# Hybrid conv / S5 / PEER layer: order of the weight tiles ahead of the experts, who issues the small inputs, where the taps stand, the conv tiles' SiLU, and when gate batches are loaded

## The chip, the cores and the metric

The kernel runs on one core of a Trainium2 chip. The metric is the device time of one execution in microseconds (us). The core has five engines, each with its own instruction stream: TensorE (PE, matmuls), VectorE (DVE), ScalarE (ACT), GpSimd (POOL) and SyncE (SP, which here only issues DMAs). They meet through semaphores only.

## The reference, cut to what matters

One layer of a decoder trunk on 512 prompt positions and 8 single-token sequences (T = 520 columns), D = 1024:

```
mods = silu(c) @ w_ada + b_ada                  # 6 x 1024, and 2 x 1024 for the final norm
h = rms_norm(x) * (1 + sc1) + sh1
a, gate, u = split(h @ w_in, [512, 1024])       # 12 tiles of 128 output rows
hc = causal_depthwise_conv(a * sigmoid(gate), width 31)
hc = silu(layer_norm(hc))
hs = glu(gelu(s5_scan(u)), w_glu)               # 32 groups, 64 complex states each
x += g1 * (concat(hc, hs) @ w_out)
h2 = rms_norm(x) * (1 + sc2) + sh2
q = h2 @ w_q; scores = q . keys                 # 8 heads x 2 x 128 keys
idx, g = top-16 of the 16 x 16 best pairs of each head
x += g2 * sum_k g_k * gelu(h2 . U[idx_k]) * V[idx_k]
y = rms_norm(x) * (1 + scf) + shf
```

The last sum is computed densely over all 16384 experts for the first 384 columns (gates are written as a table, most of them zero), and by gathered rows for the other 136.

## The kernel before

Activations lie as columns: partitions are features, the free axis is the 520 tokens. Every weight tile is 128 x 1024 f32 (512 KB) and comes through `raw`, a ring of four places. `STREAM` lists the 96 tiles ahead of the experts in the order in which SyncE asks for them: `("in", f)`, `("glu", f)`, `("out", f)`, `("q", f)` and `("ada", f)`, the modulation tiles, 16 to each of four pairs. Tile n waits until tile n - 4 has been used (`USED`): an `ada` tile when its matmuls are done, an `in`, `out` or `q` tile when its low part is computed.

Dense products are made in two parts for precision: ScalarE copies a tile rounded (`split_hi`), VectorE or GpSimd subtracts to get the rest (`split_lo`), into a ring of two (`hlm`, later `hl`), and TensorE multiplies three combinations (`split_dense`): 48 matmuls of 256 or 264 columns per tile.

The order of work ahead of the experts is written out by hand, engine by engine. The input projection (`split_dense("in", ...)`) makes 12 tiles; after tiles 1, 3, 5 and 7 it calls `modulation_rows(1, ...)` for four `ada` tiles. VectorE computes between its splits the S5 factors (`XI`, `FO`), then for each pair of gate and value tiles the GLU rows (`conv_rows`, which TensorE waits for at tiles 7, 9 and 11), and part of the 124 convolution taps (`conv_taps(count, tiles)`). After the projection come small chunk matrices (20 steps of TensorE and ScalarE), chunk inputs (`s_V`), the scan on VectorE that ends in the chunk states `S` (semaphore `s_S`), the direct chunks on TensorE, which wait for the second modulations (`s_mods`), the S5 outputs, the GLU, and on VectorE the rest of the taps. Then the layer norm: TensorE sums columns, VectorE takes reciprocals, ScalarE the root (`root("conv")`), VectorE multiplies, ScalarE applies SiLU with the permutation of columns (`natural`) and copies the rounded part (`rhi`), VectorE subtracts (`rows_lo`, into `mixin_lo`). Then the output projection, the second norm, `modulation_rows(3, ...)`, the q projection, and scores in five token tiles, which ScalarE copies from PSUM in four pieces each.

The experts: 128 tiles of U (`first_product`), then 128 of V, 16 batches of eight. For the V half SyncE loads the activations (`hring`, four places) and the gates by batches of 1.5 MB (`load_gates`, two places, `gbp`); VectorE multiplies both (`weigh`) eight tiles ahead of TensorE, and the engine's next instructions, `row_weights` (`Wd`) and `add_out`, stand behind it. Gathered activations come into `ga` with `VG` = 2 semaphores in turn.

## Time and profile before

| | before |
|---|---|
| median of 3 runs | 1979.05 us (1974.23 to 1981.84) |
| profiled execution | 1975.13 us |
| its span, first to last instruction | 1973.3 us |
| mean granted TensorE clock | 0.958 |
| busy share: PE, DVE, ACT, POOL | 90%, 61%, 35%, 34% |

The profile is that of one execution. An engine's busy share says how long it had an instruction, not whether anybody waited for it; for that one reads the chain of work that ended last, and the idle time before an instruction with what released it (`<-`). The granted clock is a share of 2.4 GHz; it has two levels, 2.4 and 1.2 GHz. PEld is the weight load, which lies beside the matmuls.

### The profile page before, as it was taken

What the parts mean: (1) busy time and instruction counts of PE and PEld (TensorE: products, weight loads), DVE (VectorE), ACT (ScalarE), POOL (GpSimd) and SP (SyncE); (2) the same over time, 40 slices, a digit from 0 to 9 for tenths busy, and PEclk for the clock granted to TensorE, in tenths of its full rate; (3) what the DMA queues carried; (4) which work ended last, traced back from release to release, by engine and by line L of the source; (5) the groups of instructions that cost most, each with busy time, mean ns of one, the idle gap of its engine ahead of it and who ended that gap; (6) DMA issues with size and microseconds to landing.
All of it is one profiled execution on the core that took longest, in us unless ns stands there. A gap on an engine that the chain in (4) does not pass through costs nothing.

```text
span 1973.3 us, 32898 instructions
## 1 busy us (share of the span) xinstructions
PE 1773.7 (90%) x13007; PEld 1640.8 (83%) x13007; DVE 1195.3 (61%) x3100; ACT 686.5 (35%) x1225; POOL 673.5 (34%) x585
## 2 busy tenths in 40 slices
PE   4578638889999999999999999998999999999996
PEld 1567526679999999999999999997788887888885
DVE  5747993304999477777676671254555554655554
ACT  1213213314333444444444443332333332333333
POOL 1010001223554533333333334464344444444300
PEclk9789868899999999999999999999999999999998
DMA  7353015443888878888888887678888888888841
GB/s 243 137 161 76 12 43 180 144 171 110 237 242 240 239 218 241 261 249 245 256 248 246 252 255 243 233 273 298 308 302 311 291 294 284 311 297 317 297 151 54
DMA packets 305705, 442.68 MB, mean 224 GB/s; under 512 B 24752, under 2 KB 221536, under 8 KB 303504
## 3 DMA queue, kind: packets, MB, share of 16 engines
q1 hardware_dynamic: 275104, 365.06, 57.8%
q0 software_dynamic: 25136, 74.24, 11.4%
q8 instruction: 103, 1.69, 0.3%
q10 hardware_dynamic: 5312, 1.29, 0.3%
q14 instruction: 50, 0.41, 0.1%
HBM read 377.37 MB, written 130.25 MB: 257 GB/s over the span
## 4 chain that ended last, share of the span: by engine, by line
PE 79%; DVE 9%; DMA 7%; ACT 2%; issue 1%; ACTq 1%; POOL 0%; SPq 0%; DVEq 0%
PE ps L1707 37%; PE ps L1734 23%; PE ps L1505 9%; DMA gbp<-gate_spill 5%; PE ps L1696 4%; PE ps L1686 3%; DVE conv_out L1108 3%; DMA raw<-in_w_ada 1%; DMA raw<-in_w_in 1%; PE ps L1479 1%; PE ps L1520 1%; PE ps L1462 1%; DVE rstd L1026 1%; DVE wf L1379 0%; ACTq L640 0%
## 5 line engine op out<-in xcount | busy, mean ns | idle before, releaser
L1707 PE MATMUL ps<-h,hl 128*128 128x256 f32 (+1 forms) x6144 | 823.7, 288 | 0.0
L1707 PEld LDWEIGHTS ps<-h,hl 128*128 128x128 f32 x6144 | 761.7, 189 | 0.2 <-ACT sc L811 0.2
L1734 PEld LDWEIGHTS ps<-WH,hl 128*128 128x128 f32 x3072 | 535.2, 188 | 41.0 <-issue 26.9
L794 ACT ACTIVATE hl<-raw 128x512 fp32r<-128x512 f32 x512 | 320.7, 629 | 706.0 <-PE ps L1707 473.5
L1734 PE MATMUL ps<-WH,hl 128*128 128x384 f32 x3072 | 550.9, 339 | 6.5 <-DVE x_res L1425 5.2
L593 POOL TENSOR_TENSOR hl<-raw,hl 128x512 fp32r<-128x512 f32 x260 | 351.7, 1354 | 496.8 <-ACT hl L794 496.4
L1418 DVE TENSOR_TENSOR hl<-raw,hl 128x512 fp32r<-128x512 f32 x252 | 173.6, 694 | 212.6 <-ACT hl L794 212.5
L601 POOL DMA_INDIRECT gathered_act<-act_spill,act_index x136 | 133.8, 984 | 261.1 <-DVE Wd L1256 226.8
L1347 DVE TENSOR_SCALAR ohA<-ps,selT 128x128 f32<-128x128 f32 x384 | 134.2, 349 | 146.2 <-PE ps L1696 133.5
L1348 DVE TENSOR_SCALAR ohB<-ps,selT 128x128 f32<-128x128 f32 x384 | 154.7, 403 | 0.0
L1696 PE MATMUL ps<-ohB,ohA 128*128 128x128 f32 x768 | 147.1, 273 | 1.5 <-DVE ohB L1348 1.5
L610 POOL DMA_INDIRECT v_rows_ring<-v_rows,v_row_index x136 | 132.7, 976 | 41.5 <-issue 41.5
L1505 PE MATMUL ps<-rows_hi,hlm 128*128 128x256 f32 (+1 forms) x640 | 115.7, 303 | 34.6 <-DVE hlm L999 22.7
L847 ACT ACTIVATE WH<-wf 128x384 fp32r<-128x384 f32 x128 | 66.8, 525 | 207.0 <-DVE wf L1379 207.0
L1505 PEld LDWEIGHTS ps<-rows_hi,hlm 128*128 128x128 f32 x640 | 97.9, 206 | 40.1 <-DVE hlm L999 37.8
L1379 DVE TENSOR_TENSOR wf<-hring,gbp 128x384 f32<-128x384 f32 x128 | 74.5, 582 | 85.6 <-DMA gbp<-gate_spill 85.0
L1696 PEld LDWEIGHTS ps<-ohB,ohA 128*128 128x128 f32 x768 | 118.9, 189 | 1.7 <-ACT selT L865 1.7
L840 ACT ACTIVATE stage<-ps 128x512 f32<-128x512 f32 x96 | 102.5, 1068 | 11.8 <-PE ps L1696 11.8
L1462 PE MATMUL ps<-raw,sil 128*32 128x512 f32 x256 | 55.4, 719 | 46.3 <-DMA raw<-in_w_ada 26.6
L1686 PE MATMUL ps<-v_rows_ring,Wd 128*32 128x512 f32 x544 | 73.0, 659 | 23.5 <-DVE Wd L1256 23.5
L1425 DVE SCALAR_TENSOR_TENSOR x_res<-ps,mods,x_res 128x384 f32<-128x384 f32 x128 | 78.3, 612 | 7.6 <-PE ps L1734 7.6
L1386 DVE TENSOR_TENSOR WH<-wf,WH 128x384 fp32r<-128x384 f32 x128 | 72.6, 568 | 17.0 <-ACT WH L847 11.7
(272 smaller groups left out, 1327.6 us busy)
## 6 DMA issues: line engine op xcount, KB each, us to landing
raw<-in_u SPq DMA_DIRECT2D x128, 512.0 KB, 6.8
v_rows<-in_v SPq DMA_DIRECT2D x128, 512.0 KB, 5.7
raw<-in_v SPq DMA_DIRECT2D x128, 512.0 KB, 6.9
act_spill<-actr SPq DMA_DIRECT2D x128, 260.0 KB, 2.6
raw<-in_w_ada SPq DMA_DIRECT2D x64, 512.0 KB, 4.6
gate_spill<-stage SPq DMA_DIRECT2D x24, 1024.0 KB, 7.6
hring<-act_spill SPq DMA_DIRECT2D x128, 192.0 KB, 4.0
gbp<-gate_spill SPq DMA_DIRECT2D x16, 1536.0 KB, 8.2
```

The costliest lines, as they stand in the source:

```text
L593: pool.tensor_tensor(hl[:, n % 2, 1, c], raw[:, n % NRAW, c], hl[:, n % 2, 0, c].bitcast(F32), ALU.subtract).then_inc(s_wlo, 1)
L601: pool.indirect_dma_start(ga[:, tok:tok + 1], None, hd.rearrange("n p (t o) -> (n p t) o", o=1), bass.IndirectOffsetOnAxis(ap=ida[:, tok:t ...
L610: pool.indirect_dma_start(vring[:, g % VG, c, :], None, vrd, bass.IndirectOffsetOnAxis(ap=idv[:, tok:tok + 1], axis=0))\
L794: act.activation(hl[:, n % 2, 0, c], raw[:, n % NRAW, c], ACT.Copy).then_inc(s_whi, 1)
L1347: dve.tensor_scalar(ohA[:, s, :], ps[:, 7, 0:P], selT[:, 0, tok:tok + 1], None, ALU.is_equal)
L1348: dve.tensor_scalar(ohB[:, s, :], ps[:, 7, 0:P], selT[:, 1, tok:tok + 1], selT[:, 2, tok:tok + 1], ALU.is_equal, ALU.mult).then_inc(s_oh, 1)
L1418: dve.tensor_tensor(hl[:, n % 2, 1, c], raw[:, n % NRAW, c], hl[:, n % 2, 0, c].bitcast(F32), ALU.subtract).then_inc(s_vlo, 1)
L1505: last = pe.matmul(ps[:, bank + h, 0:b - a], ring[:, k % 2, w, q * P:(q + 1) * P], rows[r][:, q, a:b], start=i == 0 and (w, r) == (0, 0), ...
L1686: last = pe.matmul(ps[32 * c:32 * c + 32, acc_bank(s) + half, :], Wd[:, g % 2, c, :], vring[:, g % VG, c, 512 * half:512 * half + 512], st ...
L1696: pe.matmul(ps[:, 4 + g % 2, i * P:(i + 1) * P], ohA[:, tok % OHR, :], ohB[:, tok % OHR, :], start=True, stop=True).then_inc(s_tok, 1)
L1707: last = pe.matmul(ps[:, 2 * (m % 2) + h, 0:b - a], hl[:, m % 2, w, q * P:(q + 1) * P], h2[:, r, q, a:b], start=q == 0 and (w, r) == (0, 0 ...
L1734: last = pe.matmul(ps[:, mm % 2, 0:ND], hl[:, mm % 2, w, j * P:(j + 1) * P], WHL[b % 2][:, r, j, :], start=j == 0 and (w, r) == (0, 0), st ...
```

## The change

1. `STREAM` is put in the order in which TensorE uses the tiles: the 12 `in` tiles in a row, then `ada` pair 1; `out` 0 and 1 after twelve tiles of pair 2.
2. `modulation_rows(1, ...)` leaves the input projection and is done in four pieces after it; its column step and VectorE's `modulations(1)` come later. `modulation_rows(2, ...)` is cut otherwise: 2, 4 and 2 of the eight steps, the last behind output tile 0.
3. The 12 loads of small inputs are issued by SyncE after the first four weight tiles, ahead of x, and no longer by ScalarE.
4. Ten taps stand before the scan (six after the skip is added, four before the wait for the chunk inputs).
5. Conv tiles: VectorE multiplies by the root's result and permutes in one step into `mixin`, ScalarE does one SiLU over 520 columns in place, and VectorE makes the rounded copy. ScalarE's splits of `out` 0 and 1 stand behind the squares and ahead of the root.
6. ScalarE's splits of `q` 0 and 1 move into the output projection's loop.
7. Scores: ScalarE copies two pieces per token tile, VectorE the other two; the first expert product waits for both.
8. Gate batch b + 3, no longer b + 2, is loaded at the end of block b of the V half, with batch 2 at its first tile.
9. Gathered activations have four semaphores and are issued one group ahead of the gathered V rows.

```diff
@@ -69,6 +69,7 @@
 VG = 2
+GA = 4
 HR = 2
@@ -95,16 +96,12 @@
     return [(kind, f) for f in indices]
-STREAM = (ada(0, 0, KD) + tiles_of("in", 8, 9)
-          + ada(1, 0, 2) + tiles_of("in", 10, 11)
-          + ada(1, 2, 4) + tiles_of("in", 0, 4)
-          + ada(1, 4, 6) + tiles_of("in", 1, 5)
-          + ada(1, 6, 8) + tiles_of("in", 2, 6, 3, 7)
+STREAM = (ada(0, 0, KD) + tiles_of("in", 8, 9, 10, 11, 0, 4, 1, 5, 2, 6, 3, 7)
+          + ada(1, 0, KD)
           + tiles_of("glu", 0, 1, 2, 3)
-          + tiles_of("out", 0, 1) + ada(2, 0, 5)
-          + tiles_of("out", 2, 3) + ada(2, 5, 8)
-          + tiles_of("out", 4, 5, 6, 7)
-          + tiles_of("q", 0, 1) + ada(3, 0, 8)
+          + ada(2, 0, 6) + tiles_of("out", 0, 1)
+          + ada(2, 6, KD) + tiles_of("out", 2, 3, 4, 5, 6, 7)
+          + tiles_of("q", 0, 1) + ada(3, 0, KD)
           + tiles_of("q", 2, 3, 4, 5, 6, 7))
@@ -451,6 +449,11 @@
                 load(n)
+            for name, t in (("par", par[:]), ("bm", bm[:]), ("cm", cm[:]), ("h0", h0[:]),
+                            ("cw", cw[:]), ("cvec", cvec[:]), ("bada", bada[:]), ("ngain", ngain[:])):
+                sp.dma_start(t, dr[name]).then_inc(s_small, 16)
+            for c in range(CT):
+                sp.dma_start(stc[:, c, :, 0:CW - 1], dr["stc"][:, c]).then_inc(s_small, 16)
             for k in range(KD):
@@ -520,9 +523,12 @@
                 b = mm // JB
-                if mm % JB == JB - 1 and b + 2 < NB:
+                if mm == 0:
+                    sp.wait_ge(s_w, JB)
+                    load_gates(2)
+                if mm % JB == JB - 1 and b + 3 < NB:
                     sp.wait_ge(s_w, JB * (b + 2))
-                    load_gates(b + 2)
+                    load_gates(b + 3)
             sp.wait_ge(s_hs, 3 * (KD + 1))
@@ -595,12 +601,12 @@
             def gather_acts(g):
-                after(pool, s_wd, g - VG + 1)
+                after(pool, s_wd, g - GA + 1)
                 for c in range(NGT):
...
                                             bass.IndirectOffsetOnAxis(ap=ida[:, tok:tok + 1], axis=0))\
-                        .then_inc(s_ga[g % VG], 16)
+                        .then_inc(s_ga[g % GA], 16)
             def gather_v(g, c):
@@ -626,18 +632,15 @@
                 gather_v(0, c)
+            gather_acts(1)
             for g in range(1, NGG):
-                gather_acts(g)
+                if g + 1 < NGG:
+                    gather_acts(g + 1)
                 for c in range(NGT):
...
         def _(act):
-            for name, t in (("par", par[:]), ("bm", bm[:]), ("cm", cm[:]), ("h0", h0[:]),
-                            ("cw", cw[:]), ("cvec", cvec[:]), ("bada", bada[:]), ("ngain", ngain[:])):
-                act.dma_start(t, dr[name]).then_inc(s_small, 16)
-            for c in range(CT):
-                act.dma_start(stc[:, c, :, 0:CW - 1], dr["stc"][:, c]).then_inc(s_small, 16)
             act.wait_ge(s_c, 16)
@@ -698,8 +701,6 @@
                 last.then_inc(s_sig, 1)
-                if t == 2:
-                    modulation_rows(1)
             for e in range(20):
@@ -719,6 +720,8 @@
                                    ps[:, 3 * a + b, 0:(t1 - t0) * (NC + 2 * TS)], ACT.Copy).then_inc(s_Ve, 1)
+            modulation_rows(1)
+
             def chunk_outputs(e):
@@ -746,22 +749,18 @@
                 last.then_inc(s_gsig, 1)
+            act.wait_ge(s_hsm, CT)
+            act.activation(rhi[:, CT:KD, :], mixin[:, CT:KD, :], ACT.Copy).then_inc(s_rh, 1)
+
+            act.wait_ge(s_cvd, 1)
+            squares("conv", cv, CT)
             split_hi(FSP["out"], hlm)
             split_hi(FSP["out"] + 1, hlm)
-            act.wait_ge(s_hsm, CT)
-            act.activation(rhi[:, CT:KD, :], mixin[:, CT:KD, :], ACT.Copy).then_inc(s_rh, 1)
-
-            act.wait_ge(s_cvd, 1)
-            squares("conv", cv, CT)
             root("conv")
...
                 act.wait_ge(s_cn, t + 1)
-                act.activation(mixin[:, t, 0:TP].rearrange("p (i c) -> p i c", i=L), natural(cv[:, t, 0:TP]), ACT.Silu,
-                               scale=cvec[:, 1, t:t + 1], bias=cvec[:, 2, t:t + 1])
-                act.activation(mixin[:, t, TP:T], cv[:, t, TP:T], ACT.Silu,
+                act.activation(mixin[:, t, :], mixin[:, t, :], ACT.Silu,
                                scale=cvec[:, 1, t:t + 1], bias=cvec[:, 2, t:t + 1]).then_inc(s_hcm, 1)
-                act.wait_ge(s_hcm, t + 1)
-                act.activation(rhi[:, t, :], mixin[:, t, :], ACT.Copy).then_inc(s_rh, 1)
             for k in range(KD):
@@ -771,10 +770,10 @@
                 act.activation(sq[:, k % 2, :], x[:, k, :], ACT.Square).then_inc(s_sq, 1)
-                if k == 5:
+                if k == 3:
                     modulation_rows(2)
-            split_hi(FSP["q"], hl)
-            split_hi(FSP["q"] + 1, hl)
+                if k in (5, 6):
+                    split_hi(FSP["q"] + k - 5, hl)
             root("rms2")
@@ -806,7 +805,7 @@
                 act.wait_ge(s_sc, t + 1)
-                for q in range(4):
+                for q in range(2):
                     part, h4 = divmod(q, 2)
@@ -1124,7 +1123,6 @@
             conv_rows(3)
-            modulations(1)
             for i in range(5):
@@ -1135,6 +1133,7 @@
                 dve.scalar_tensor_tensor(lag0, mask, cvec[:, 3, n4:n4 + 1], lag0, ALU.mult, ALU.add).then_inc(s_dg, 1)
+            conv_taps(6, tuple(range(CT)))
             prod = wt[:, :, :].rearrange("p t c -> p (t c)")[:, 0:CT * TS * CW].rearrange(
@@ -1153,6 +1152,7 @@
                 cmul([R[:, a, :, m:2 * m] for a in (0, 1)], q, [R[:, a, :, 0:m] for a in (0, 1)], wt[:, :, 0:m])
+            conv_taps(4, tuple(range(CT)))
             dve.wait_ge(s_Ve, 6)
@@ -1167,6 +1167,7 @@
                 link(dve.tensor_tensor_scan(W2f[:, a, :], wtf, W2f[:, a, :], 0.0, ALU.mult, ALU.add))
+            modulations(1)
             dve.tensor_tensor(V[:, 0, :, 0:NC], W2[:, 0], R[:, 0], ALU.mult)
@@ -1199,10 +1197,17 @@
             dve.wait_ge(s_cvd, 1)
-            variance("conv", CC)
+            reciprocals("conv", CC)
+            split_lo(FSP["out"])
+            dve.wait_ge(s_rstd, RSTD["conv"])
             for t in range(CT):
-                dve.tensor_tensor(cv[:, t, :], cv[:, t, :], rstd[:], ALU.mult).then_inc(s_cn, 1)
+                dve.tensor_tensor(mixin[:, t, 0:TP].rearrange("p (i c) -> p i c", i=L), natural(cv[:, t, 0:TP]),
+                                  natural(rstd[:, 0:TP]), ALU.mult)
+                dve.tensor_tensor(mixin[:, t, TP:T], cv[:, t, TP:T], rstd[:, TP:T], ALU.mult).then_inc(s_cn, 1)
+            split_lo(FSP["out"] + 1)
             for t in range(CT):
+                dve.wait_ge(s_hcm, t + 1)
+                dve.tensor_copy(rhi[:, t, :], mixin[:, t, :]).then_inc(s_rh, 1)
                 rows_lo(t, t + 2)
@@ -1242,13 +1247,26 @@
             dve.wait_ge(s_h2l, KD + 1)
+
+            def scores_half(t):
+
+                dve.wait_ge(s_sc, t + 1)
+                for q in range(2, 4):
+                    part, h4 = divmod(q, 2)
+                    last = dve.tensor_copy(sc[0:size(t), t, 8 * h4 + part:8 * h4 + 8:2, :],
+                                           ps[0:size(t), 4 * (1 - t % 2) + q, :].rearrange("p (a n) -> p a n", n=NK))
+                last.then_inc(s_scd, 1)
+
+            for t in range(NTT):
+                scores_half(t)
             dve.wait_ge(s_act, NTT)
+            dve.wait_ge(s_scd, NTT)
             dve.memset(Wd[:], 0.0)
...
             def row_weights(g):
-                dve.wait_ge(s_ga[g % VG], 16 * NGT * (g // VG + 1))
+                dve.wait_ge(s_ga[g % GA], 16 * NGT * (g // GA + 1))
                 if g >= 2:
@@ -1532,14 +1550,8 @@
             modulation_columns(0)
-            def second_modulations(t):
-
-                if t % 2 and t < 8:
-                    modulation_rows(1, t - 1, t + 1)
-                if t == 9:
-                    modulation_columns(1)
-
-            split_dense("in", hlm, (rhi, h1lo), None, s_win, second_modulations)
+            split_dense("in", hlm, (rhi, h1lo), None, s_win)
+            modulation_rows(1, 0, 2)
             pe.wait_ge(s_Xr, 3)
@@ -1566,6 +1578,8 @@
                 last.then_inc(s_prep, 1)
+                if e == 15:
+                    modulation_rows(1, 2, 4)
             pe.wait_ge(s_prepe, 20)
@@ -1578,15 +1592,24 @@
             last.then_inc(s_V, 1)
+            modulation_rows(1, 4, 6)
+
             def chunk_out(t, g):
                 return ps[0:NC + TS, 4 * g + t // 4, (t % 4) * P:(t % 4 + 1) * P]
+            def direct_chunks(g, first, last_):
+
+                for t in range(first, last_):
+                    pe.matmul(chunk_out(t, g), U[:, 2 * t + g, 0:NC + TS], Tm[:, 2 * t + g, :], start=t % 4 == 0, stop=False)
+
             pe.wait_ge(s_Ve, 6)
+            direct_chunks(0, 0, ST)
+            modulation_rows(1, 6, KD)
+            direct_chunks(1, 0, ST // 2)
+            modulation_columns(1)
             pe.wait_ge(s_mods, 2)
-            for g in range(2):
-                for t in range(ST):
-                    pe.matmul(chunk_out(t, g), U[:, 2 * t + g, 0:NC + TS], Tm[:, 2 * t + g, :], start=t % 4 == 0, stop=False)
+            direct_chunks(1, ST // 2, ST)
             pe.wait_ge(s_S, 1)
@@ -1623,17 +1646,17 @@
                 last.then_inc(s_glu, 1)
-            modulation_rows(2, 0, 1)
+            modulation_rows(2, 0, 2)
             pe.wait_ge(s_cv, CT * CW)
...
             column_sums(sq_rows, CT, SQ_BEFORE["conv"], True)
-            modulation_rows(2, 1, 5)
+            modulation_rows(2, 2, 6)
             def third_modulations(t):
-                if t == 3:
-                    modulation_rows(2, 5, KD)
-                if t == 6:
+                if t == 0:
+                    modulation_rows(2, 6, KD)
+                if t == 4:
                     modulation_columns(2)
@@ -1712,6 +1736,7 @@
                         token(slot_token(m, q))
+            pe.wait_ge(s_scd, NTT)
             for m in range(NK):
```

The three places that matter most, as the instructions stand on the engines. First SyncE's queue ahead of the experts, before; each row is an instruction form with its count, `raw<-in_w_ada` a modulation tile, `raw<-in_w_in` an input projection tile.

```order
L448 DMA raw<-in_w_ada 128x1024 x12
L448 DMA raw<-in_w_in 128x1024 x2
L448 DMA raw<-in_w_ada 128x1024 x4
L448 DMA raw<-in_w_in 128x1024 x2
...
L448 DMA raw<-in_w_ada 128x1024 x4
L448 DMA raw<-in_w_in 128x1024 x4
L448 DMA raw<-in_w_glu 128x512 x4
L448 DMA raw<-in_w_out 128x1024 x2
L448 DMA raw<-in_w_ada 128x1024 x10
L448 DMA raw<-in_w_out 128x1024 x2
L448 DMA raw<-in_w_ada 128x1024 x6
L448 DMA raw<-in_w_out 128x1024 x4
```

The same queue in the changed kernel, from its beginning.

```order
L446 DMA raw<-in_w_ada 128x1024 x4
...
L454 DMA ngain_sb<-in_ngain 128x24
L456 DMA stc_sb<-in_stc 128x8x30 x4
L458 DMA x_res<-in_x 128x520 x8
L446 DMA raw<-in_w_ada 128x1024 x12
L446 DMA raw<-in_w_in 128x1024 x12
L446 DMA raw<-in_w_ada 128x1024 x16
L446 DMA raw<-in_w_glu 128x512 x4
L446 DMA raw<-in_w_ada 128x1024 x12
L446 DMA raw<-in_w_out 128x1024 x2
L446 DMA raw<-in_w_ada 128x1024 x4
L446 DMA raw<-in_w_out 128x1024 x6
```

The input projection's tiles stand in one row of 12, the eight small inputs and `stc` between the first weights and x, and the first two output tiles behind twelve modulation tiles.

Second ScalarE at the conv layer norm, before: `uT` is the GLU's sigmoid, `hlm<-raw` the split of an output tile, `sq` the squares, `rstd` the root, `mixin` the SiLU.

```order
L747 ACTIVATE uT<-ps 128x264
L655 ACTIVATE hlm<-raw 128x1024 x2
L752 ACTIVATE rows_hi<-mixin 128x2080
L661 ACTIVATE sq<-conv_out 128x520 x4
L665 ACT_TABLE_LOAD
L665 ACTIVATE rstd<-rstd 128x520
L759 ACT_TABLE_LOAD
L759 ACTIVATE mixin<-conv_out,cvec_sb 128x512
L761 ACTIVATE mixin<-conv_out,cvec_sb 128x8
L764 ACTIVATE rows_hi<-mixin 128x520
```

And in the changed kernel.

```order
L750 ACTIVATE uT<-ps 128x264
L753 ACTIVATE rows_hi<-mixin 128x2080
L664 ACTIVATE sq<-conv_out 128x520 x4
L658 ACTIVATE hlm<-raw 128x1024 x2
L668 ACT_TABLE_LOAD
L668 ACTIVATE rstd<-rstd 128x520
L762 ACT_TABLE_LOAD
L762 ACTIVATE mixin<-mixin,cvec_sb 128x520 x4
```

The two splits have moved from ahead of the norm to between the squares and the root, and three instructions per conv tile have become one.

## Rows read from the trace of the kernel before

**Rows 1.** The page, part 4: the chain by line, shares of the span.

```profile
PE ps L1707 37%; PE ps L1734 23%; PE ps L1505 9%; DMA gbp<-gate_spill 5%; PE ps L1696 4%; PE ps L1686 3%; DVE conv_out L1108 3%; DMA raw<-in_w_ada 1%; DMA raw<-in_w_in 1%; PE ps L1479 1%; PE ps L1520 1%; PE ps L1462 1%; DVE rstd L1026 1%; DVE wf L1379 0%; ACTq L640 0%
```

**Rows 2.** Timeline (start, us, instruction) and DMA queues (packets, MB, share), 0 to 22 us.

```profile
5.21 12.69 ACTq L640 DMA_DIRECT2D stc_sb<-in_stc  x4
20.17 0.17 DVE L919 TENSOR_SCALAR K<-par_sb 128x16 f32<-128x16 f32 x1 [20.17 <-DMA stc_sb<-in_stc]
...
q1 hardware_dynamic: 1872, 4.26, 53.8%
q10 hardware_dynamic: 5312, 1.29, 30.2%
```

**Rows 3.** The chain in order of time, and one window, in the input projection.

```profile
67.04 14.39 PE ps L1505 x96
...
82.46 3.60 DMA raw<-in_w_in
...
170.28 11.51 PE ps L1505 x96
...
67.00:181.80 114.80, 89.83 (x648) 82.94 (x652) 66.79 (x88) 16.46 (x27) 10.79 (x18) 0.84 0.45 138
```

**Rows 4.** Timeline of VectorE and ScalarE, 183 to 287 us.

```profile
183.59 0.18 DVE L1089 TENSOR_TENSOR stc_sb<-ps,sq 128x8 f32<-128x8 f32 x1
...
226.78 59.72 DVE L1108 SCALAR_TENSOR_TENSOR conv_out<-hc,cw_sb,conv_out 128x512 f32<-128x512 f32 x90
...
253.57 2.00 ACT L655 ACTIVATE hlm<-raw 128x1024 fp32r<-128x1024 f32 x2
```

**Rows 5.** Timeline, 302 to 319 us, from the column sums to the low rows.

```profile
302.57 0.76 DVE L1024 TENSOR_SCALAR rstd<-ps 128x256 f32<-128x256 f32 x2 [4.08 <-PE ps L1520]
...
306.80 0.64 ACT L665 ACTIVATE rstd<-rstd 128x520 f32<-128x520 f32 x1 [5.15 <-DVE rstd L1026]
...
307.56 1.09 PE L1462 MATMUL ps<-raw,sil 128*32 128x512 f32 x4 [3.25 <-DMA raw<-in_w_ada]
...
308.69 2.42 SPq L448 DMA_DIRECT2D raw<-in_w_out  x2
308.75 1.34 ACT L759 ACTIVATE mixin<-conv_out,cvec_sb 128x512 f32<-128x512 f32 x1
...
317.79 0.70 DVE L1197 TENSOR_TENSOR mixin_lo<-mixin,rows_hi 128x520 fp32r<-128x520 f32 x1 [1.58 <-ACT rows_hi L764]
```

**Rows 6.** The chain in order of time, in the output projection.

```profile
337.70 1.07 PE ps L1462 x8
...
347.33 2.35 POOL hlm L556
...
351.82 6.26 PE ps L1505 x48
```

**Rows 7.** Timeline, DMA issues (KB each, median us to landing) and chain, 380 to 412 us.

```profile
381.31 1.06 PE L1462 MATMUL ps<-raw,sil 128*32 128x512 f32 x8
...
raw<-in_w_ada SPq DMA_DIRECT2D x14, 512.0 KB, 4.8
...
410.20 46.35 PE ps L1505 x384
```

**Rows 8.** V half: a wait (total, times, longest), chain, window, landing of raw tiles.

```profile
DVE wf L1379 <- DMA gbp<-gate_spill: 60.1, 14, 8.7
...
1343.29 3.29 PE ps L1686 x16
1346.58 12.67 PE ps L1734 x72
1359.25 1.85 PE ps L1686 x16
...
1296.30:1952.00 655.70, 623.73 (x3653) 555.72 (x3654) 368.06 (x709) 217.04 (x381) 267.27 (x273) 0.98 0.78 278
...
DMA to landing us min/median/max: 3.5/7.2/12.8
```

10 lines of the change are left out of this document (5 added, 5 removed).

## The prediction

> **What bounds the kernel now.** I began with the chain by line [rows 1]: TensorE's own lines hold most of it, but a DMA, `gbp<-gate_spill`, stands there with 5% of the span. That is no arithmetic, so it is a place to look. Then I cut the span into stretches and asked of each what ends last.
>
> Start (0 to 67 us). ScalarE's queue spends 12.69 us on issuing the four `stc` loads, and VectorE's first instruction waits for the last of them until 20.17 us [rows 2]. From there VectorE works almost without a gap until TensorE's first input-projection tile at 67.04: the start is 20.17 plus VectorE's own chain.
>
> Input projection (67.04 to 181.79). The chain shows a pattern that comes four times: two tiles on TensorE in about 14.4 us, four modulation tiles, then a weight tile that is only now being fetched (3.60 us), its two splits, and TensorE again. The last pair, which nothing interrupts, takes 11.51 us, the first 14.39 [rows 3]: after each gap TensorE runs at its lower clock for a while. The stretch is 114.8 us long with TensorE's mean clock at 0.84, and VectorE is busy for 66.79 of it [rows 3].
>
> Then VectorE alone: from the last GLU rows at 183.6 to the chunk states (`S`, about 226) and on through 90 taps in 59.72 us (0.664 each), to 286.5, while ScalarE had done the GLU's last sigmoid and gone on to its splits at 253.57 [rows 4]. Taps are the end of this stretch, and every microsecond that VectorE loses in the input projection returns here.
>
> After the taps: column sums, root, SiLU, split, and TensorE resumes after the last `mixin_lo`, at 318.5 [rows 5]. The output projection stops once more, for six modulation tiles and a weight tile behind them with its splits, from 337.7 to 351.8 [rows 6]. Then 16 modulation tiles pass through the ring of four from 381.31 to 410.2 [rows 7].
>
> The first expert half (to 1296) has no gap worth naming. The second (1296.3 to 1952.0): TensorE is busy 623.73 of 655.70 us at clock 0.98; VectorE waits 14 times for a gate batch, 60.1 us in all; behind that wait stands `Wd`, for which TensorE waits, and after it 16 row-sum matmuls take 3.29 us where they else take 1.85 [rows 8].
>
> **The change, part by part.**
>
> *Small inputs by SyncE.* The 12 loads leave ScalarE's queue and stand on SyncE's behind four weight tiles and before x. What counts is when the last `stc` lands, since VectorE's chain starts there. In the first 22 us ScalarE's queue used 30.2% of the 16 engines, 6.6 us of full use, and SyncE's 53.8%, 11.8 us for 4.26 MB [rows 2]. Now x no longer competes: first 2.1 MB of weights (half of 11.8 = 5.9), then 6.6, from about 2.5 us: 15 us if nothing is lost in between. If on SyncE's queue the four issues take their 12.69 us again, behind the others from about 8 us on, it is 23 instead of 20.2. I take -3 us (bounds -5 and +4). SyncE's next weights leave after x, where TensorE would wait for them at worst until VectorE's reciprocal needs it; cover is 8 us.
>
> The Trainium skill (DMA: Bandwidth & Descriptors, "Queues, rings and completion order") says that SyncE and ScalarE each have a ring of their own on the same 16 engines, which take turns between rings and go through one ring in order. By that rule `stc` now waits for all weights ahead of it and gets no turns of its own; with the skill's companion rule that spreading over issuers saves only issue time ("Issuing engines are not separate DMA queues") the total work is unchanged, which would put the start between no change and my -3. No row here has `stc` alone in a ring.
>
> *Weights in order of use, input projection.* The modulation tiles between the pairs go behind it, so the ring of four always holds the next tiles: each is asked for when the one four before it is split, three tiles (17 us) ahead, against 3.6 us to land. First pair 14.39 (cold start stays), then ten tiles at 11.51/2 = 5.76: 72.0 us, end at 139.0 instead of 181.8: -42.8. VectorE must keep up: its 66.79 us of work stand in the same 72. Following its order through, I find it continuously busy from about 106 us, and TensorE's waits for the GLU rows at tiles 7, 9 and 11 met with under 1 us to spare. So up to 6 us may be lost; if the cover is gone, VectorE's splits are late next. I take -42.8 (bounds -36, -43).
>
> *Modulation pair 1 and taps.* Pair 1 is now multiplied in pieces where TensorE waits: 16 tiles of some 0.5 us each [rows 7], fetched behind each other with 4 to 9 us per four, all before `S` is there. VectorE's ten moved taps cost 10 x 0.664 wherever they are; they stand before `S`, so `S` and the GLU come 6.6 us later relative to the taps. The GLU ends 27.7 us after `S` (253.6 - 226), and the 82 remaining taps take 54.4: cover 27 us. Only the 0.7 us wait is filled. Taps end 43 us earlier.
>
> *After the taps.* Here the change adds a wait. The first two output tiles now stand behind twelve modulation tiles. In the page's own terms: after the column sums at 302.5 four modulation tiles are at hand, the next four land from 307.56 on, and only the use of the first of these frees the place for an output tile, at 308.69 [rows 5]. It lands about 4.2 us later (313; between the 3.60 of [rows 3] and the 4.8 of [rows 7]), the second 1.2 us after. ScalarE's two splits of them now stand *ahead* of its root (1.0 us each, [rows 4]), so the root ends near 317.1 instead of 307.4: +9.7. Against that: before, each conv tile cost ScalarE 2.26 us (308.75 to 317.79 for four), and the last `mixin_lo` was done at 318.5, 11 us after the root; now there is one SiLU per tile, which VectorE outlasts: four multiplications (each the 0.70 of a subtraction and a small piece, 3.1), one split (twice as long, 1.3), then copy and subtraction per tile (0.35 to 0.70 for the copy, which no row shows; 0.70): 8.5 us after the root, at 325.7. TensorE, idle and cold, ends output tile 0 about 8 us later than before.
> Then the output projection no longer stops for six modulation tiles: the gap from 337.7 to 351.8 (some 12 us besides the work in it) shrinks to about 1 us for the four now behind tile 0, and some 1.5 us for output tile 2 (fetched late, split on GpSimd in 2.35). Net at its end: -2.
> Modulation pair 3: its first four tiles are already there (the splits of q 0 and 1 moved ahead), twelve come through the ring at 4.8 us to landing [rows 7], 5.6 to 6.6 us per four: 22 to 25 us instead of 28.9. TensorE's q projection follows the last modulation tile at once [rows 7], so nothing else holds it. With the -2, the q projection starts 6 to 9 us earlier. I take -8 for the whole tail (bounds -12 and +4).
>
> *Scores.* TensorE was the slower side there, so halving ScalarE's share gains almost nothing, and the first expert product now waits for VectorE's copy of the last tile from PSUM: VectorE took 0.76 for 520 elements from PSUM [rows 5], so two of 512 some 1.3. +1 (bounds 0, +1.5).
>
> *Gate batches.* Before, batch b+2 is asked for at the end of block b and needed one tile later: 14 waits of 4.3 us in the mean [rows 8]. Now batch b+3 is asked for there, and needed eight tiles (38 us) later. The wait of VectorE goes wholly. TensorE at full clock: 24 matmuls in 12.67/3 = 4.22, 128 x 4.22 = 540.6; 34 row sums x 1.85 = 62.9; final sums and transposes, 36 small matmuls and two waits for copies, I put at 9: 612.5 against 655.7, so 43 us are waits and the lower clock behind them. I take -41; if only the idle 32 less the copies' waits came back, -28. The earlier gathers (four activation buffers) move nothing: no row waits for a gather.
> Order on SyncE: the raw tile right behind a gate batch already lands last, at most 12.8 us after its issue [rows 8]; it is needed about 15 us after it, and its split 5 us later still.
>
> **Sum.** -3 - 43 - 8 + 1 - 41 = -94. The profiled execution took 1975.1 us (span 1973.3); the median of the runs is 3.9 above it. 1975.1 - 94 + 3.9 = 1885.
>
> **Rivals.**
> 1. *As summed*, 0.58: 1885, own range 1872 to 1898.
> 2. *Only idle time comes back in the second expert half*, or raw tiles behind gate batches are late by about 1 us each: -28 instead of -41. For it: DMA is already 0.78 busy there [rows 8], and less time must carry the same bytes. Against: the landing times. 1898. 0.14.
> 3. *VectorE bounds the input projection*: three late GLU rows and a cold clock after each: -36, with the start at +4: 1885 + 7 + 7 = 1899. For it: margins under 1 us. 0.13.
> 4. *The root behind the late output tiles costs more*: landing at 6 us rather than 4.2, then a second gap at output tile 2: tail +4 instead of -8: 1897. 0.12.
> 5. *Slower*: the gate batch of 1.5 MB, no longer waited for, holds back every raw tile behind it. It starts to cost when such a tile lands over 20 us after issue (15 plus the 5 of cover) and turns the total round only if TensorE then stops for 7 us at each of 15 batches (94/15 + 0.5): landing at 27 us against 12.8 now; about 1995. 0.01.
> 6. *The order does nothing* because VectorE, not the weights, sets the pace: then only the gates count, 1885 + 43 + 5 = 1933. Against: each gap in [rows 3] names the weight DMA. 0.02.
>
> A measurement of this kernel can tell about 0.5% (10 us) from no change. Cases 1 to 4 are all faster by far; two of them together give about 1912. Range 1866 to 1912: the lower end takes -5, -12, -43, -43. Faster 0.97, same 0.02, slower 0.01.
>
> **What would show it.** VectorE's first instruction near 17 us; input projection as 12 tiles without a DMA in the chain, 72 us; taps ending near 240; the root some 10 us later after the conv column sums than before, and named as waiting for output weights; no gap after output tile 3; no `gbp` wait behind the first block, and row sums all at 1.9 us with the second expert half at 613 to 615 us. Wrong it would be if `gbp` waits stay, if conv rows wait for VectorE with idle TensorE at tiles 7 to 11, or if the start lies beyond 24 us.

## The result, and the profile after

The changed kernel takes 1884.14 us in the median of four runs (1880.45 to 1886.38), the kernel before 1976.89 on the same chip (four runs, 1974.23 to 1981.84): ratio 0.9526, 95% interval 0.9499 to 0.9553. The prediction was 1885 us. The profiled execution took 1882.85 us, its span is 1881.0 (before 1973.3): 92.3 us less. Mean granted clock 0.97.

The chain by line of the changed kernel, to be held against [rows 1] (only the largest shares are printed):

```profile
PE ps L1731 39%; PE ps L1759 28%; PE ps L1523 8%; PE ps L1720 5%; PE ps L1710 3%; DVE conv_out L1107 3%; DMA raw<-in_w_ada 2%; PE ps L1480 1%; PE ps L1497 1%; PE ps L1538 1%; DMA v_rows_ring<-v_rows,v_row_index 1%; DMA raw<-in_w_out 0%; PE ps L1679 0%; DVE rstd L1025 0%; ACT v_rows_ring L673 0%
```

`gbp<-gate_spill` is gone from it and `raw<-in_w_in` too. `raw<-in_w_ada` has grown, and `raw<-in_w_out`, which stood in the chain before with one load of 6.16 us, has two now (5.51 and 3.88). `v_rows_ring<-v_rows` is new: TensorE's first row sums wait 1.6 us for the first gathered rows. Stage by stage:

**Start** (timelines of SyncE and VectorE, changed kernel; [rows 2] are those of before):

```profile
7.59 4.52 SPq L456 DMA_DIRECT2D stc_sb<-in_stc  x4
14.96 0.17 DVE L918 TENSOR_SCALAR K<-par_sb 128x16 f32<-128x16 f32 x1 [14.96 <-DMA stc_sb<-in_stc]
```

The four issues take 4.52 us instead of 12.69, VectorE starts 5.2 us earlier, and the input projection begins as much earlier (61.83 against 67.04).

**Input projection** (chain, and one window with its columns PE, PEld, DVE, ACT, POOL busy, granted clock, DMA share, GB/s; [rows 3] before):

```profile
61.83 71.36 PE ps L1523 x576
...
61.80:133.20 71.40, 71.37 (x580) 71.26 (x584) 66.75 (x88) 16.22 (x26) 10.79 (x18) 0.97 0.45 119
```

Twelve tiles are one piece of the chain. VectorE's busy time is that of before (66.75 against 66.79), in a window 43.4 us shorter.

**To the end of the taps** (timelines of TensorE and VectorE; [rows 4] before):

```profile
152.08 1.92 PE L1480 MATMUL ps<-raw,sil 128*32 128x512 f32 x4 [4.04 <-DMA raw<-in_w_ada]
...
165.78 1.22 DVE L1158 TENSOR_TENSOR mixin<-V,mixin 128x1024 f32<-128x1024 f32 x1 [3.91 <-ACT V L721]
...
186.64 54.41 DVE L1107 SCALAR_TENSOR_TENSOR conv_out<-hc,cw_sb,conv_out 128x512 f32<-128x512 f32 x82
```

A wait that the prediction did not have: TensorE, on its way to the chunk inputs, stops for the last tile of a modulation step, and VectorE waits 3.91 us ahead of the scan (before, its one wait there was 0.73). Taps end at 241.10, 45.4 earlier, although the end of the input projection came 48.6 earlier.

**Tail** (chain, column sums to output tile 2, then ScalarE's splits of output tiles 0 and 1 from its timeline; [rows 5, 6] before):

```profile
250.94 5.32 PE ps L1538 x16
256.25 1.02 PE ps L1480 x8
257.27 3.78 DMA raw<-in_w_ada
...
264.28 5.51 DMA raw<-in_w_out
...
272.19 0.65 ACT rstd L668
...
272.86 1.13 DVE mixin L1204
...
279.54 5.39 PE ps L1523 x24
284.93 1.02 PE ps L1480 x8
285.95 3.88 DMA raw<-in_w_out
...
291.06 2.40 POOL hlm L562
```

```profile
267.34 1.06 ACT L658 ACTIVATE hlm<-raw 128x1024 fp32r<-128x1024 f32 x1 [12.28 <-DMA raw<-in_w_out]
269.81 1.06 ACT L658 ACTIVATE hlm<-raw 128x1024 fp32r<-128x1024 f32 x1 [1.42 <-DMA raw<-in_w_out]
```

The root ends 16.6 us after the column sums (256.25 to 272.84); before, it was 4.9 (302.5 to 307.44). Between them stand two loads: the modulation tiles nine to twelve, for whose first TensorE waits, then output tile 1, whose place only the second of these frees (output tile 0 lands 2.5 us ahead of it, at 267.3). VectorE's last low row comes 9.9 us after the root. The load and the splits of output tile 2 fill 7.5 us of the chain, but TensorE makes output tile 1 in that time and itself waits 0.77 us. From the end of the taps to the q projection, which starts at 358.69, it is 117.6 us against 123.65.

**Scores and experts.** From the q projection to the first V tile 886.3 us against 886.1. In the V half (window; then the group of the row sums, busy and mean ns, idle and releaser; then the landing of raw tiles; [rows 8] before):

```profile
1245.00:1860.20 615.20, 610.31 (x3655) 551.87 (x3656) 368.32 (x710) 218.76 (x381) 282.31 (x273) 1.00 0.80 296
...
L1710 PE MATMUL ps<-v_rows_ring,Wd 128*32 128x512 f32 x544 | 65.4, 598 | 1.6 <-DMA v_rows_ring<-v_rows,v_row_index 1.6
...
DMA to landing us min/median/max: 3.4/5.4/10.8
```

No wait for a gate batch is left in this window, the granted clock is 1.00, and raw tiles land sooner than before, not later (10.8 us at most against 12.8).

### The profile page after: what moved, and what is told of

It reads as the page before. It is cut to its first block, busy times and chain, and to the rows that moved or that the text cites. A ratio compares the mean times of both kernels' runs of the same rounds, so it can differ in the third digit from the quotient of the medians.

```text
span 1881.0 us, 32902 instructions
## 1 busy us (share of the span) xinstructions
PE 1755.2 (93%) x13007; PEld 1631.8 (87%) x13007; DVE 1200.5 (64%) x3118; ACT 678.8 (36%) x1207; POOL 689.0 (37%) x585
## 4 chain that ended last, share of the span: by engine, by line
PE 86%; DVE 7%; DMA 3%; ACT 1%; issue 1%; SPq 1%; POOL 1%; DVEq 0%; POOLq 0%; ACTq 0%
PE ps L1731 39%; PE ps L1759 28%; PE ps L1523 8%; PE ps L1720 5%; PE ps L1710 3%; DVE conv_out L1107 3%; DMA raw<-in_w_ada 2%; PE ps L1480 1%; PE ps L1497 1%; PE ps L1538 1%; DMA v_rows_ring<-v_rows,v_row_index 1%; DMA raw<-in_w_out 0%; PE ps L1679 0%; DVE rstd L1025 0%; ACT v_rows_ring L673 0%
## 5 line engine op out<-in xcount | busy, mean ns | idle before, releaser
L1759 PE MATMUL ps<-WH,hl 128*128 128x384 f32 x3072 | 544.9, 337 | 1.3 <-ACT actr L825 1.3
L607 POOL DMA_INDIRECT gathered_act<-act_spill,act_index x136 | 152.0, 1118 | 43.5 <-issue 41.4
L1523 PE MATMUL ps<-rows_hi,hlm 128*128 128x256 f32 (+1 forms) x640 | 110.0, 293 | 20.5 <-DVE h_lo L1063 10.7
L1523 PEld LDWEIGHTS ps<-rows_hi,hlm 128*128 128x128 f32 x640 | 93.1, 197 | 23.5 <-DVE hlm L998 15.8
L1404 DVE TENSOR_TENSOR WH<-wf,WH 128x384 fp32r<-128x384 f32 x128 | 72.5, 567 | 17.0 <-ACT WH L846 11.7
L825 ACT ACTIVATE actr<-ps 128x256 f32<-128x256 f32 (+1 forms) x256 | 82.7, 374 | 0.0
```

Of the source, the lines that this page charges most:

```text
L607: pool.indirect_dma_start(ga[:, tok:tok + 1], None, hd.rearrange("n p (t o) -> (n p t) o", o=1), bass.IndirectOffsetOnAxis(ap=ida[:, tok:t ...
L1523: last = pe.matmul(ps[:, bank + h, 0:b - a], ring[:, k % 2, w, q * P:(q + 1) * P], rows[r][:, q, a:b], start=i == 0 and (w, r) == (0, 0), ...
L1759: last = pe.matmul(ps[:, mm % 2, 0:ND], hl[:, mm % 2, w, j * P:(j + 1) * P], WHL[b % 2][:, r, j, :], start=j == 0 and (w, r) == (0, 0), st ...
```

## Experiments

The ratio compares each with the kernel before on the same chip. There its median was 1975.57 us (b_gates, a_small_act, a_v_early, a_mod2_whole), 1979.37 (a_small_first, a_in_old, a_act_copy, both_orders) or 1977.52 (the other four), against 1976.89 beside the changed kernel. "Against the changed kernel" is the difference of medians from 1884.14; the kernel before differs by up to 3.8 us between the chips, so places of a few us are read from the traces.

| run | median us | ratio to before (95%) |
|---|---|---|
| b_gates | 1932.64 | 0.9783 (0.9758 to 0.9807) |
| a_in_old | 1920.32 | 0.9699 (0.9673 to 0.9725) |
| a_small_act | 1889.75 | 0.9568 (0.9543 to 0.9592) |
| a_small_first | 1879.84 | 0.9491 (0.9464 to 0.9518) |
| a_v_early | 1878.99 | 0.9510 (0.9486 to 0.9533) |
| a_margin | 1881.97 | 0.9530 (0.9498 to 0.9562) |
| a_mod2_whole | 1870.02 | 0.9463 (0.9437 to 0.9490) |
| a_act_copy | 1883.81 | 0.9518 (0.9493 to 0.9543) |
| a_no_scores_gathers | 1883.51 | 0.9524 (0.9501 to 0.9547) |
| both_orders | 1864.80 | 0.9424 (0.9399 to 0.9450) |
| combined | 1856.22 | 0.9387 (0.9365 to 0.9410) |
| combined_woven | 1851.07 | 0.9364 (0.9342 to 0.9386) |

**The gates alone** (the kernel before with this one edit)

```diff
+                if mm == 0:
+                    sp.wait_ge(s_w, JB)
+                    load_gates(2)
-                if mm % JB == JB - 1 and b + 2 < NB:
+                if mm % JB == JB - 1 and b + 3 < NB:
                     sp.wait_ge(s_w, JB * (b + 2))
-                    load_gates(b + 2)
+                    load_gates(b + 3)
```

> The kernel before with one edit of the change alone: gate batch b+3 loaded at the end of block b of the V half, batch 2 at its first tile. Theory (the prediction's term: waits and the lower clock behind them both come back): -41 us against the kernel before, second expert half 615 us, VectorE's waits for gate batches (60.1 us over 14 waits) all gone, row sums all near 1.9 us. Rival (only idle time comes back): -28 us, TensorE still at a lower clock in places. Second rival (the gain in the whole change needs the other edits of the V half too, the four activation buffers): less than -28, with waits for gathers in place of the gate waits.

1932.64 us, 42.9 below before. Its V half (same columns as above):

```profile
1292.00:1909.30 617.30, 611.48 (x3651) 551.92 (x3652) 367.75 (x709) 218.95 (x381) 265.04 (x273) 1.00 0.81 295
```

617.3 us against 655.7, with TensorE at full clock throughout: 38.4 less here. The other 4.1 of the profiled execution's 42.5 lie ahead of this window, where nothing was changed, and are not the edit's. Idle time alone (28) is out, and so is the need for the other edits of the V half.

**The input projection's old order**

```diff
-          + ada(1, 0, KD)
+          + ada(1, 0, 2) + tiles_of("in", 10, 11)
+          + ada(1, 2, 4) + tiles_of("in", 0, 4)
...
-            split_dense("in", hlm, (rhi, h1lo), None, s_win)
-            modulation_rows(1, 0, 2)
+            split_dense("in", hlm, (rhi, h1lo), None, s_win, second_modulations)
...
```

> The changed kernel with the second modulations' tiles back between the pairs of input projection tiles, in the queue and on TensorE; the column step and VectorE's part of it stay where the change has them. Theory (the term of the prediction, waits for weight tiles and a cold clock after each): the input projection takes 115 us instead of 71.4, +43; and since the fourth-last chunk matrices then wait for no modulation tile, VectorE's 3.9 us wait ahead of the scan is gone: +40 in all against the changed kernel. Rival (VectorE sets the pace of this stretch, so that its ten moved taps and not the order gave part of the gain): +36 or less.

+36.2 us. The window of the input projection in this run, then VectorE's splits (busy, mean ns, idle before them) from 100 to 240 us, in this run and, in the second view, in the changed kernel:

```profile
61.70:173.90 112.20, 88.42 (x644) 81.73 (x648) 66.38 (x88) 15.98 (x26) 10.82 (x18) 0.84 0.46 142
...
L1001 DVE TENSOR_TENSOR hlm<-raw,hlm 128x1024 fp32r<-128x1024 f32 x8 | 9.8, 1222 | 32.6 <-ACT hlm L661 32.6
```

```profile
L998 DVE TENSOR_TENSOR hlm<-raw,hlm 128x1024 fp32r<-128x1024 f32 x5 | 6.1, 1219 | 0.6 <-ACT hlm L658 0.6
```

The stretch is 40.8 us longer, 4.0 come back at the scan, and 36.6 arrive at the end of the taps. The total stands where the rival's line was drawn, but by the theory's parts: 40.8 for 43, and 4.0 for 3 at the scan. What the order gave is seen in the second row: in the changed kernel VectorE no longer stands idle for 32 us behind splits of tiles that are being fetched. The ten moved taps are moved in this run as well, so they gave none of these 36.6. That what counts here is VectorE's time, the next run tests.

**More taps where TensorE waits for VectorE**

```diff
-            conv_taps(6, (0,))
+            conv_taps(16, (0,))
             split_lo(FSP["in"] + 9)
```

> The changed kernel with ten more taps (6.6 us of VectorE) ahead of the split of input projection tile 9 and the second GLU rows, and ten fewer behind the chunk states. In the changed kernel the second GLU rows end at 114.4 and TensorE needs them near 115.4, so it must now wait 5 to 6 us there. Theory (from 100 us on VectorE is the bound, and TensorE's waits in the input projection cost nothing as long as VectorE has work): TensorE's input projection takes 77 us instead of 71.4, and the taps end where they did; whole time within 2 us. Rival (the prediction's third rival: late GLU rows cost what TensorE waits, and a cold clock behind it): +5 us or more.

TensorE's wait, the whole window, and the taps behind the chunk states:

```profile
122.46 0.77 PE L1523 MATMUL ps<-rows_hi,hlm 128*128 128x256 f32 x2 [6.45 <-DVE stc_sb L1088]
...
62.00:142.30 80.30, 73.83 (x580) 73.53 (x584) 74.15 (x97) 16.21 (x26) 10.82 (x18) 0.93 0.41 106
...
192.32 47.78 DVE L1107 SCALAR_TENSOR_TENSOR conv_out<-hc,cw_sb,conv_out 128x512 f32<-128x512 f32 x72
```

TensorE loses 6.45 us there and its input projection takes 80.3 us, 8.9 more, yet the taps end at 240.1 (changed kernel: 241.1) and the time is 1881.97. So VectorE's work is the bound here, and TensorE's wait doesn't reach the end. The test is a little kinder than it looks: VectorE waits only 0.49 us ahead of the scan instead of 3.91, and of these 3.4 us the taps' end keeps 1.0. Some 2.4 us went elsewhere, about 1.2 of them (an estimate: ten taps at 0.12 more each) into ten more taps in a row on one tile, and 0.8 into waits behind ScalarE's splits (1.4 in all, 0.6 in the changed kernel).

**Small inputs: back on ScalarE, and first on SyncE**

```diff
+                act.dma_start(t, dr[name]).then_inc(s_small, 16)      # a_small_act, all 12
...
```

> The changed kernel with the 12 small inputs back on ScalarE's queue. Theory (the whole of the earlier start comes from them): VectorE's first instruction near 20.2 us instead of 14.96, the first input projection tile near 67 instead of 61.83, and the whole time +5 us against the changed kernel, since everything up to the GLU rows hangs on VectorE. Rival (the start came earlier, but what follows has slack): the start moves by 5 us and the whole time by less than 2.

VectorE starts at 20.25 and the input projection at 67.11, 5.3 later: as expected. The taps end only 2.5 us later, behind a modulation tile that took 15.16 us to land and not 16.50; the q projection starts 0.5 later (359.23 against 358.69), the profiled span is 1.9 longer, and the medians differ by 5.6. That the start moved is shown; how much of it reaches the end is not settled by this run, and the rival is not out.

```diff
+            (the 12 small loads)                                      # a_small_first
             for n in range(NRAW):
                 load(n)
-            (the 12 small loads)
...
```

> The changed kernel with the 12 small inputs ahead of the first four weight tiles on SyncE's queue, not behind them. In the changed kernel's trace VectorE's first instruction waits for the last stc load until 14.96 us, and from there to the first input projection tile at 61.83 VectorE works without a gap. Theory (the start is the landing of stc plus VectorE's chain): stc lands near 10 us, the input projection begins 4.5 to 5 us earlier, the whole time -4.5 us against the changed kernel. Rival: the first weight tiles come later by as much, TensorE's sixteen modulation tiles (last one at 46 us) then hold the first modulations, and the input projection begins less than 1.5 us earlier.

```profile
10.44 0.17 DVE L918 TENSOR_SCALAR K<-par_sb 128x16 f32<-128x16 f32 x1 [10.44 <-DMA stc_sb<-in_stc]
...
57.26 71.01 PE ps L1523 x576
```

VectorE, the input projection and the end of the taps (236.6) all come 4.5 us earlier, the median is 4.3 lower. The first weights, later by the small loads, hold nobody.

**One modulation step out of the way of the chunk inputs**

```diff
                 if e == 15:
-                    modulation_rows(1, 2, 4)
+                    modulation_rows(1, 2, 3)
...
-            modulation_rows(1, 4, 6)
+            modulation_rows(1, 3, 6)
```

> The changed kernel, with one of the second modulations' eight steps moved: only step 2 stands behind the sixteenth chunk matrix, step 3 behind the chunk inputs. Theory: TensorE's 4.04 us wait for that step's last tile is what made VectorE wait 3.91 us for the chunk inputs ahead of the scan; now the chunk inputs are copied near 159 us, VectorE doesn't wait, and taps, column sums and all behind come 3.9 us earlier: -4 us. Rival: the wait moves to the second modulations, for which VectorE waits behind the scan (tiles fetched later), and the time stays within 1 us of the changed kernel.

```profile
161.83 1.22 DVE L1158 TENSOR_TENSOR mixin<-V,mixin 128x1024 f32<-128x1024 f32 x1
...
182.76 54.34 DVE conv_out L1107 x82
```

VectorE goes from its taps into the scan without a wait, the taps start 4.0 us earlier with the input projection 0.55 later, the q projection 3.3 earlier, and the median is 5.2 lower (3.8 if each is measured from the kernel before on its own chip). The rival's wait for the second modulations did not appear. But in this execution the tile that had been late landed 7.4 us after its issue at the latest, so the wait might have been gone without the edit. The two last runs below settle it: there a tile of this group takes 17.5 and 19.6 us to land, later than the chunk inputs begin (at 145.6 and 145.1), and VectorE still goes into the scan without a wait.

**Third modulations ahead of the column sums**

```diff
-          + ada(2, 0, 6) + tiles_of("out", 0, 1)
-          + ada(2, 6, KD) + tiles_of("out", 2, 3, 4, 5, 6, 7)
+          + ada(2, 0, KD) + tiles_of("out", 0, 1, 2, 3, 4, 5, 6, 7)
...
-            modulation_rows(2, 0, 2)
+            modulation_rows(2, 0, KD)
...
```

> The changed kernel with all eight steps of the third modulations (pair 2) ahead of the conv column sums, in the 22 us in which TensorE waits for taps, and the output tiles behind them in one row. Theory (the late root and the gap at output tile 2 are both the weights' order): output tiles 0 and 1 have landed before the sums, the root ends 5.7 to 6 us after the column sums instead of 16.6, no gap at output tile 2, q projection starts 18 us earlier relative to the end of the taps (117.6 becomes about 100): -18 us. Rival: twelve modulation tiles take longer than the 22 us (5 us to land for each ring of four, 15 to 20 us in all), the column sums start late by up to 3 us: -15. Second rival: the root is held by VectorE's or ScalarE's own work and not by the output tile: -8.

The timelines of TensorE and ScalarE at the sums and the root, and the chain behind:

```profile
237.59 1.05 PE L1479 MATMUL ps<-raw,sil 128*32 128x512 f32 x4 [1.30 <-DMA raw<-in_w_ada]
240.34 3.77 PE L1537 MATMUL ps<-conv_out,ones 128*128 128x256 f32 x16 [1.70 <-DVE conv_out L1106]
...
255.50 0.64 ACT L667 ACTIVATE rstd<-rstd 128x520 f32<-128x520 f32 x1 [2.35 <-DVE rstd L1024]
...
266.48 12.52 PE ps L1522 x102
279.00 0.88 PE ps L1496 x4
279.88 5.76 PE ps L1522 x48
```

The last modulation tile is done 1.7 us before the last tap, the sums wait for taps only. The root ends 5.0 us after the sums (251.17 to 256.14) and waits for VectorE's reciprocal, and TensorE makes output tiles 0 to 7 without a gap once the low rows are there. Taps to pair 3: 75.2 us against 95.0. Pair 3 itself then took 26.8 us instead of 22.6, so 15.6 of the expected 18 are left; the median is 14.1 lower. The first rival's -15 is what came, but not by its mechanism, since the column sums were not late; the second is out.

**Rounded copies back on ScalarE**

```diff
+                act.wait_ge(s_hcm, t + 1)
+                act.activation(rhi[:, t, :], mixin[:, t, :], ACT.Copy).then_inc(s_rh, 1)
...
```

> The changed kernel with the rounded copy of the four conv tiles back on ScalarE behind each SiLU (the multiplication with the permutation stays on VectorE, the SiLU stays one instruction). From the changed kernel's trace: the root ends at 272.84, VectorE's four multiplications take 1.07 each, its split 1.14, and copy and subtraction 1.05 per tile, the last one ends at 282.7, 9.9 us after the root. Theory: VectorE is the longer side of this stretch, so the copy moved away ends it at ScalarE's 4 x 1.3 behind the first multiplication, near 7 us after the root: -2.8 us. Rival: ScalarE becomes the longer side by its waits between SiLU and copy, no gain.

VectorE's split of output tile 1 and its four subtractions, which now follow each other:

```profile
275.64 1.23 DVE L1000 TENSOR_TENSOR hlm<-raw,hlm 128x1024 fp32r<-128x1024 f32 x1
276.78 2.54 DVE L1197 TENSOR_TENSOR mixin_lo<-mixin,rows_hi 128x520 fp32r<-128x520 f32 x4
```

The last low row comes 8.0 us after the root instead of 9.9: -1.9 where -2.8 was expected, because VectorE's own work (multiplications, a split, four subtractions) still fills the stretch. In the whole time nothing shows (-0.3): the chunk states came 1.6 us later in this execution, behind a modulation tile that took 18.96 us to land and not 16.50. Locally confirmed, by the median inconclusive.

**Scores and gathers as before**

```diff
-                for q in range(2):
+                for q in range(4):
...
-GA = 4
+GA = 2
...
```

> The changed kernel with two of its edits undone: ScalarE copies all four pieces of the scores again, and gathered activations have two semaphores and no lead. Theory (the prediction's terms): +1 for the scores with a bound of 0 to 1.5 and 0 for the gathers, so that undoing both gives between -1.5 and 0 us; the only gather wait in the second expert half of the changed kernel is 1.9 us at its first row sums. Rival (with the gate waits gone, TensorE reaches the gathers earlier, and their lead is what hides them): waits for gathered rows or activations at several of the 34 groups, +3 us or more.

1883.51 us, -0.6. Scores to the first expert product take 10.34 us here and 10.55 in the changed kernel, and the only wait of the row sums for gathered rows is one of 1.9 us (1.6 in the changed kernel). The rival is out; both edits are worth nothing that can be measured.

**Edits together**

> The changed kernel with two edits together, each run alone before: one step of the second modulations behind the chunk inputs, and all third modulations ahead of the conv column sums. Alone they gave -5 and -14 us against the changed kernel. Theory (they lie behind each other in time and share nothing): -18 to -20 us, about 1865. Rival (with the taps ending 4 us earlier the 16 modulation tiles no longer fit ahead of the column sums): the sums wait for a weight tile by up to 3 us, -15 to -17.

1864.80, -19.3, as the theory had it; TensorE's last modulation tile is done 2.8 us ahead of the last tap, so the rival is out. Then three more edits with these two:

```diff
+            for t in range(CT):
+                rows_lo(t, t + 2)
             split_lo(FSP["out"] + 1)          # combined: the edits of four runs above, and this move
-            for t in range(CT):
...
-                rows_lo(t, t + 2)
```

> The changed kernel with the edits of five runs together: small inputs first in SyncE's queue, one step of the second modulations behind the chunk inputs, all third modulations ahead of the conv column sums, rounded copies of the conv tiles on ScalarE, and VectorE's split of output tile 1 behind the conv tiles' low rows. Theory (the gains lie behind each other on one path): both orders gave 1864.8 us; the start -4.5, the copies -2 and the split's place -1: about 1857 to 1859. Rival (with the start 4.5 us earlier the modulation tiles don't fit ahead of the column sums any more, since TensorE's 16 tiles had 2.8 us to spare): 1860 or more, with the sums waiting for a weight tile.

1856.22: just below the theory's 1857 to 1859. The column sums wait for taps only, with 3.2 us to spare, so the rival is out; what each of the three added edits gave is not read apart. Then pair 3, half of it between output tiles:

```diff
+          + ada(2, 0, KD) + tiles_of("out", 0, 1, 2) + ada(3, 0, 1) + tiles_of("out", 3)
+          + ada(3, 1, 2) + tiles_of("out", 4) + ada(3, 2, 3) + tiles_of("out", 5)
+          + ada(3, 3, 4) + tiles_of("out", 6, 7)
...
+                if 1 <= t < 5:
+                    modulation_rows(3, t - 1, t)
...
```

> The combined kernel with half of the fourth modulations (pair 3, eight of 16 tiles) woven into the output projection, two behind each of the output tiles 1 to 4, and the second step of the third modulations (columns) ahead of the output projection. Theory: the stretch from the last column sum to the q projection is held by the fetching of 12 tiles through the ring of four (23.6 us in the run with both orders), while VectorE has the first normed rows after 12 us: with 8 tiles left it takes 12 to 13 us, and the eight woven tiles cost TensorE 0.52 us each, 4.2 in all: -7 us against the combined kernel, about 1850. Rival: an output tile behind woven modulation tiles is fetched too late for its split, TensorE waits 2 us at each of four, and the gain is gone.

The chain ahead of the q projection, in the combined kernel and in the woven one:

```profile
308.67 4.99 DMA raw<-in_w_ada
...
318.08 5.28 DMA raw<-in_w_ada
...
324.49 4.96 DMA raw<-in_w_ada
...
330.54 14.49 PE ps L1522 x119
```

```profile
310.36 3.41 DVE rstd L1027
313.80 0.64 ACT rstd L669
...
315.21 5.30 DVE h2f L1041 x8
...
321.46 23.55 PE ps L1523 x194
```

The loads have left the chain and the norm's own work stands in it. Taps to q projection: 89.6 us against 98.2 (changed kernel 117.6), and TensorE waits for no output tile behind a woven modulation tile, so the rival is out. 1851.07 us: 5.2 below the combined kernel, where 7 were expected and the traces of this stretch show 8.6; 33 below the changed kernel, and the fastest here.

## Why the prediction was right, and where its steps were off

The total was met within 1 us, and the mechanisms of the two large terms were right: the weights' order and the gate batches gave 84 of the 92 us, each within 1 us of its term. That the sum is as near is partly luck. The small terms were off by -2.2, +3.2, +1.9 and -0.8 us, which nearly cancel, and the median lies 1.3 us above the profiled execution and not 3.9, which takes back the other 2. The range was not well derived at its lower end: the terms that it names (-5, -12, -43, -43) make about 1876, not 1866.

- *Small inputs*, -3 predicted: -5.2 measured, just outside the term's bounds (-5 and +4). The sum behind it was right, "15 us if nothing is lost in between" against 14.96; what was mis-sized is the allowance for the issue on SyncE, which took 4.52 us and not 12.69. The last `stc` was issued 3.5 us earlier (11.40 against 14.87) and landed 3.54 us behind its issue instead of 5.27. The Trainium skill (DMA: Bandwidth & Descriptors, "Issuing engines are not separate DMA queues") says that issuing from several engines saves only issue time, and that this is usually small beside the DMA. Here it was not small: the four `stc` took 12.69 us to issue, and moving them to the engine that issues the weights made that shorter; the reading drawn from the page, no change to -3, did not hold. Whether the order in the ring gave part of the further 4.5 us in the run with the small loads first is not shown: `stc` was issued 4.6 us earlier there and landed as long behind its issue as in the changed kernel (3.58 against 3.54).
- *Input projection*, -42.8: -43.4. The twelve tiles took 71.4 us, 72.0 predicted. The margin of under 1 us for the GLU rows held, with no wait of TensorE. But "So up to 6 us may be lost" named a risk that was hardly one: with such a wait made on purpose (6.45 us) the taps ended no later. The third rival, at 0.13, put a price on waits that this run does not show; the sixth, that the order does nothing, is out with the run of the old order.
- *Modulation pair 1 and taps*, 0 predicted: +3.2. This step failed. "Pair 1 is now multiplied in pieces where TensorE waits", "all before `S` is there", looked at the end of the stretch, and not at what stands behind the pieces on TensorE: four chunk matrices and the chunk inputs, for which VectorE waits: 3.91 us instead of 0.73. With one step moved away the wait is gone, also where the tile is as late as here (the two combined runs).
- *Tail*, -8: -6.1. The late root was foreseen with its cause, at +9.7; it was +11.7. Output tile 0 landed 4.3 us after its issue, as predicted (4.2). But its place came free 0.8 us later than allowed, since the modulation tile before it was multiplied at a lower clock behind TensorE's wait (mean granted clock 0.69 from 261 to 266 us, matmuls of 1.06 us where others take 0.59), and output tile 1 took 5.51 us to land, so that it came 2.5 us behind tile 0 and not 1.2. VectorE's stretch behind the root was 9.9 us and not 8.5: the multiplication with the permuted read takes 1.08 us per tile with its small piece, not 0.78. So output tile 0 ended 10.7 us later relative to the taps, not 8. From there on the sum was right: the rest of the output projection took 10.5 us less (51.2 against 61.7, predicted -10), and pair 3 took 22.6 us (in the range of 22 to 25) instead of 28.9. The fourth rival named the late root, but its second gap did not come: TensorE waited 0.77 us at output tile 2, 1.5 allowed.
- *Scores*, +1: +0.2, with all of the first expert half in the number. TensorE waits 1.38 us for VectorE's copy, and its two short waits for ScalarE between token tiles are gone.
- *Gate batches*, -41: -41.0 by the traces of the whole change (677.0 to 636.0 from the first V tile to the end), and 38.4 in the V half where the edit stood alone (42.9 in its medians, with 4.1 that its trace places ahead of the V half). Waits and lower clock both came back. The second and the fifth rival fall with it: raw tiles landed after 10.8 us at most.

Sum: -5.2 - 43.4 + 3.2 - 6.1 + 0.2 - 41.0 = -92.3, the difference of the spans.

What made that last tile of pair 1 late can be read, but was not tried. In the chain its load takes 16.50 us, in the other runs with this order and this wait 15.2 to 19.0, but in the two runs with only this step moved, or this and pair 2, the slowest of its four took 7.4 and 9.9; here the three tiles issued with it landed after 3.7 to 7.2. The DMA view of the changed kernel from 133 to 153 us (queues with packets, MB, share of the 16 engines; then issues with KB each and median us to landing):

```profile
q1 hardware_dynamic: 639, 2.36, 45.9%
q0 software_dynamic: 224, 0.55, 44.7%
...
raw<-in_w_ada SPq DMA_DIRECT2D x7, 512.0 KB, 9.3
out_conv_s<-stc_sb POOLq DMA_DIRECT2D x4, 120.0 KB, 14.8
```

And the queues from 142.5 to 150 us alone:

```profile
q0 software_dynamic: 115, 0.28, 94.7%
q1 hardware_dynamic: 21, 0.07, 11.3%
```

GpSimd stores the conv state (q0) as soon as the last GLU rows are there. These stores take as large a share of the engines for 0.55 MB as SyncE's weights (q1) for 2.36 MB, and from 142.5 to 150 us, with the tile outstanding, they hold nearly all of the engines and the weights move 0.07 MB. The load is the stores' own: in the kernel before, where no weights move beside them (183 to 203 us), they take 41.1% of the engines over 20 us for the same 0.55 MB. That fits them as the cause; but that the tile would land in time without them, and that stored later they would cost nothing, no run here shows: in the run with the step moved the same stores ran, and the tile was not late. The moved step only took away who waits for it.
